# Two more raw weight tiles, a later wait and another order of splits in the first chunk of the last stage

## What is computed

```python
def _merge(x, oa, za, ob, zb, ga, gb, gate, w_br_a, w_br_b, w_out):
    ya = (oa * jax.nn.silu(za)) @ w_br_a
    yb = (ob * jax.nn.silu(zb)) @ w_br_b
    h = jax.nn.sigmoid(ga) * ya + jax.nn.sigmoid(gb) * yb
    return x + gate * (h @ w_out)
...
y_prompt = _rmsnorm(xp) * final_norm_g
y_sample = _rmsnorm(xs) * final_norm_g
```

## Time and profile before

| | |
|---|---|
| median of 3 runs | 1214.68 us (1213.4 to 1214.84) |
| the profiled execution's own time | 1214.08 us |
| its span (first to last instruction) | 1212.3 us |
| PE busy | 1187.5 us, 98% |
| DVE busy | 819.3 us, 68% |
| ACT busy | 601.3 us, 50% |
| POOL busy | 92.4 us, 8% |

### The profile page before, as it was taken

How to read it: one execution, slowest core, us unless ns; L and a number is a source line. 1 busy time by engine, 2 the same in 40 slices (tenths; PEclk the granted TensorE clock), 3 DMA queues, 4 the chain that set the end, 5 groups by cost and what they waited for, 6 DMA issues and landing times.

```text
span 1212.3 us, 19668 instructions
## 1 busy us (share of the span) xinstructions
PE 1187.5 (98%) x7432; PEld 1076.8 (89%) x7432; DVE 819.3 (68%) x1596; ACT 601.3 (50%) x1205; POOL 92.4 (8%) x108
## 2 busy tenths in 40 slices
PE   7999999999999999999999999999999999999998
PEld 1799889989998998899899899989989988998996
DVE  4769458656765776587687597688779966454453
ACT  4632335535552654365465455555547675344342
POOL 0000000000000000000000000000000034533430
PEclk9999999999999999999999999999999999999999
DMA  9547702141123215022511121411113376642540
GB/s 362 178 175 226 231 30 72 45 135 61 40 79 96 64 40 162 22 72 69 139 63 46 49 63 41 134 39 58 38 40 124 113 233 211 204 152 95 201 146 35
DMA packets 71762, 132.81 MB, mean 110 GB/s; under 512 B 6774, under 2 KB 47734, under 8 KB 71676
## 3 DMA queue, kind: packets, MB, share of 16 engines
q1 hardware_dynamic: 57420, 109.70, 28.0%
q10 hardware_dynamic: 14256, 21.96, 5.0%
HBM read 96.24 MB, written 35.40 MB: 109 GB/s over the span
## 4 chain that ended last, share of the span: by engine, by line
PE 84%; DVE 9%; ACT 3%; issue 2%; DMA 1%; POOL 0%; ACTq 0%; SPq 0%; DVEq 0%
PE d_ps_pairs L84 23%; PE s_ps_pairs L84 12%; PE y_ps L1881 9%; PE o_ps_pairs L1070 9%; PE b_ps L84 8%; PE t_ps_pairs L1040 7%; PE v_ps L84 6%; PE s_ps_pairs L1004 4%; PE s_ps_pairs L1003 4%; DMA wada<-in_w_ada 1%; DVE pt L1401 1%; PE k_ps L352 1%; DVE mn L1407 1%; PE t_ps L344 1%; DVE q L1392 1%
## 5 line engine op out<-in xcount | busy, mean ns | idle before, releaser
L84 PE MATMUL d_ps_pairs<-h,wt 128*128 128x384 f32 (+2 forms) x1920 | 352.2, 338 | 0.9 <-ACT craw L1212 0.9
L84 PEld LDWEIGHTS d_ps_pairs<-h,wt 128*128 128x128 f32 x1920 | 316.7, 189 | 16.4 <-ACT craw L1212 1.9
L1401 DVE TENSOR_TENSOR pt<-t_ps_pairs,pt 128x512 fp32r<-128x512 f32 (+2 forms) x264 | 152.9, 619 | 64.7 <-ACT pt L1170 63.5
L84 PE MATMUL s_ps_pairs<-h,wt 128*128 128x512 f32 (+1 forms) x864 | 168.2, 354 | 0.0
L84 PEld LDWEIGHTS s_ps_pairs<-h,wt 128*128 128x128 f32 x864 | 141.6, 189 | 21.7
L1170 ACT ACTIVATE pt<-t_ps_pairs 128x512 fp32r<-128x512 f32 (+2 forms) x264 | 130.2, 544 | 16.8 <-PE t_ps_pairs L1040 11.5
L1194 ACT ACTIVATE pr<-s_ps_pairs,mx 128x896 f32<-128x896 f32 (+1 forms) x128 | 125.0, 982 | 26.9 <-DVE mx L1429 26.5
L1040 PE MATMUL t_ps_pairs<-ident_sb,pr 128*128 128x128 f32 x928 | 125.6, 274 | 1.9 <-DVE pt L1401 1.1
L1881 PE MATMUL y_ps<-wo,mg 128*128 128x512 f32 (+1 forms) x504 | 113.2, 385 | 0.0
L1040 PEld LDWEIGHTS t_ps_pairs<-ident_sb,pr 128*128 128x128 f32 x928 | 105.4, 140 | 8.8 <-DVE pt L1401 5.8
L1881 PEld LDWEIGHTS y_ps<-wo,mg 128*128 128x128 f32 x504 | 91.3, 188 | 20.6
(11 more groups left out here) (204 smaller groups left out, 1588.0 us busy)
## 6 DMA issues: line engine op xcount, KB each, us to landing
wraw<-in_w_gate SPq DMA_DIRECT2D x24, 512.0 KB, 3.8
gt<-gates_d SPq DMA_DIRECT2D x40, 256.0 KB, 4.5
gates_d<-craw ACTq DMA_DIRECT2D x48, 192.0 KB, 1.9
v_d<-vst SPq DMA_DIRECT2D x20, 320.0 KB, 4.6
wada<-in_w_ada SPq DMA_DIRECT2D x12, 512.0 KB, 9.8
oz<-gates_d SPq DMA_DIRECT2D x20, 256.0 KB, 4.6
oz<-o_d SPq DMA_DIRECT2D x20, 256.0 KB, 4.3
x_f<-in_x SPq DMA_DIRECT2D x10, 512.0 KB, 7.0
```

The source lines that it names most:

```text
L84: mm = eng.matmul(out, lhs(a, k), rhs(b, k), start=(k == 0 and i == 0), stop=(k == n_k - 1 and i == 2))
L1401: dve.tensor_tensor(pt[:, 1, c * 512:c * 512 + cols], t_ps[:, n % 2, 0:cols], pt[:, 0, c * 512:c * 512 + cols].bitcast(F32), ALU.subtract) ...
```

## The change

The staging buffers become six: tiles 6 and 7 go into two new ones, `under[:, 1, :]` and `under[:, 3, :]`, which lie over `mg`: the high and the low parts of j = 4 to 7. `stage_of`, `stage_count` and `stage_before` say which buffer a tile has, which load of that buffer it is, and which tile had it before. Tiles 8 to 11 follow tiles 2 to 5, and 12 to 15 follow 8 to 11. SP issues tiles 6, 7 and 8 ahead of the loop, after a new wait for `o_done` (the end of DVE's last work of `pairs`). The wait for the last store moves from before the loop to within j = 4, behind tile 9. In the loop tile 2j + 1 stands ahead of gate tile j and tile 2j + 2 behind it. The lists of splits by turn differ. `gate_in` and `gain_in` share semaphores with the two new buffers, so their counts start one higher.

```diff
+def stage_of(m):
+    return m - 2 if m < 8 else m % 4
+def stage_count(m):
+    return 1 if m < 8 else m // 4
+def stage_before(m):
+    return m - 6 if m < 12 else m - 4
...
 def weight_raw(f, m):
-    return f["stage"][(m - 2) % 4]
+    return f["stage"][stage_of(m)]
...
 def tile_high_f(act, f, m):
-    act.wait_ge(f["w_in"][(m - 2) % 4], ((m - 2) // 4 + 1) * 16)
+    act.wait_ge(f["w_in"][stage_of(m)], stage_count(m) * 16)
...
-    EXTRA = [[4], [5, 6], [7], [8, 9], [10], [11, 12], [13], [14, 15]]
+    EXTRA = [[4], [5], [6], [7, 8], [9, 10], [11, 12], [13, 14], [15]]
...
         def load_w(m):
-            if m >= 6:
-                wait_split(sp, f, m - 4)
+            if m >= 8:
+                wait_split(sp, f, stage_before(m))
...
         load_gt(0, 3)
+        sp.wait_ge(o_done, ALL * STEPS)
         load_w(6)
-        sp.wait_ge(o_out, PAIRS * 32 + 16)
+        load_w(7)
+        load_w(8)
 
         def body(i, first, last):
             for j in range(GSLOTS, KD):
                 if first:
-                    load_w(2 * j - 1)
-                    load_w(2 * j)
+                    load_w(2 * j + 1)
+                    if j == GSLOTS:
+                        sp.wait_ge(o_out, PAIRS * 32 + 16)
                 load_gt(i, j)
+                if first and j < KD - 1:
+                    load_w(2 * j + 2)
             if first:
-                load_w(WT - 1)
...
-                dve.wait_ge(gain_in, 16)
-            dve.wait_ge(gate_in, (i + 1) * 16)
+                dve.wait_ge(gain_in, 32)
+            dve.wait_ge(gate_in, (i + 2) * 16)
...
+        with ExitStack() as early:
+            under = sb(early, "under_mg", [P, 4, D])
         own_f["mg"] = sb(ctx, "mg", [P, 2, KD, CT], F32R)
...
-        own_f.update(wb=wb, wo=wo, stage=[x[:, 0, :], x[:, 1, :], wraw[:, :], craw[:, :]])
+        own_f.update(wb=wb, wo=wo, stage=[x[:, 0, :], x[:, 1, :], wraw[:, :], craw[:, :], under[:, 1, :], under[:, 3, :]])
```

More of the change, by code:

```diff
@@ L1625, in finish_tables @@
     f = dict(own)
-    f["w_in"] = [sem(f"w_in{s}") for s in range(4)]
+    f["w_in"] = [sem(f"w_in{s}") for s in range(6)]
     f["first_in"] = [sem(f"first_in{n}") for n in range(PIECES)]
@@ L1657, in finish @@
     x_in, y_out = [sem("x_in0"), sem("x_in1")], [sem("y_out0"), sem("y_out1")]
-    gate_in, gain_in, eps_set = sem("gate_in"), sem("gain_in"), sem("eps_set")
+    eps_set = sem("eps_set")
+    gate_in, gain_in = w_in[4], w_in[5]
     y_mm, gated, res, sq_done, rms_done, r_done, y_done = (
@@ L1681, in load_w @@
         def load_w(m):
-            if m >= 6:
-                wait_split(sp, f, m - 4)
+            if m >= 8:
+                wait_split(sp, f, stage_before(m))
             src = io["w_br"][m] if m < KD else io["w_out"][:, m - KD, :]
-            sp.dma_start(weight_raw(f, m), src).then_inc(w_in[(m - 2) % 4], 16)
+            sp.dma_start(weight_raw(f, m), src).then_inc(w_in[stage_of(m)], 16)
         def load_oz(i, n):
```

## The result

The changed kernel takes 1220.24 us (median of 6, 1217.58 to 1220.79) against 1214.53 us for the kernel before (6 runs, 1213.24 to 1214.95): +5.7 us, ratio 1.0045 with a 95% interval of 1.0035 to 1.0055. Its profiled execution took 1219.88 us, the span 1218.1.

The account below looks back on a forecast made before the run. TensorE, busy 1187.5 of 1212.3 us, was taken to bound the kernel. The gate-tile loop delays its k=7 by 5.8 us, other parts priced at zero: 1214.68 + 5.8 = 1220.5 us, range 1215.5 to 1224.7.

Parts of the forecast that it names:

- The term that counts: Last stage, chunk 0: gate tiles behind weights that wait for later splits form a serial loop; PE's k=7 +5.8 us.
- Gate 5 lands: Landing of gate tile 5 in chunk 0, taken at 995.0, between 993.5 and 996.5; it was 994.8 before.
- First turn: Gate 5 through sigmoid 5, split 9 and weight 13 to gate 6 landed: 7.2 us, landing at 1002.2.
- Second turn: Gate 6 through sigmoid 6, split 11 and weight 15 to gate 7 landed: 7.2 us, landing at 1009.4.
- Sigmoid 7 to the last low part: Chunk 0, j=7: two splits ahead of product 7 instead of one, so 7.9 us in place of 6.9.
- mg_lo(7) done: Low part of chunk 0's last merged product, done at 1017.4; PE's k=7, which needs it, was at 1011.6.
- signs named for "right": PE waits 1.5 to 2 us before j=6; gates 6, 7 issued near 998, 1005.5; ACT waits over 3; y_ps stops 4 to 6.
- First half of the splits: Chunk 0's branch pass: the 0.88 us wait before j=4 goes and reappears at j=6, gain zero.
- The long sum on GpSimd: GpSimd's sum for j=7 in chunk 0 keeps its long 1.65 us beside a split; short price would give +4.9.
- The moved store wait: SP's `o_out` wait, moved to j=4, costs nothing: it ended by 982.4, when gate tile 4's product ended anyway.
- The early loads: Tiles 6 to 9 issued earlier by SP, but sharing one stream, so landings come earlier only by a little.
- rival "faster": Loads arrive in time, PE loses nothing at k=7: 1212.2 to 1213.8 us, if gate 5 lands by 989.3; chance 0.07.

Follow-up runs that it names:

- e1: Changed kernel with gate tiles 5 to 7 put back ahead of weights 2j+1 and 2j+2 in SyncE's order: 1214.16 us.
- e5: Changed kernel with gate tile 7 alone moved ahead of weight 15 in SyncE's order: 1215.84 us.
- e6: Changed kernel with gate tile 6 alone moved ahead of weight 13 in SyncE's order: 1217.35 us.
- e2: Kernel before with the new order of splits alone, four buffers and SyncE's old order: 1217.05 us.
- x2: Changed kernel with gate tiles first and the old order of splits throughout, keeping six buffers and early loads: 1214.37 us.
- e10: Changed kernel with gate 5 behind weight 10, gates 6 and 7 behind weight 11, ahead of weights 12 to 15, and splits a turn later: 1212.64 us.
- e11: Changed kernel with gate 5 behind weight 10, gates 6 and 7 behind weight 11, ahead of weights 12 to 15, keeping its own splits: 1212.66 us.
- e4: Changed kernel with 16 matmuls added ahead of the wait for k=5 in chunk 0's output pass: 1219.81 us.
- e9: Kernel before with the new order of splits, plus 16 matmuls added ahead of j=7 in chunk 0: 1216.01 us.
- e3: Changed kernel with the old order of splits alone: 1219.42 us.

## Why the prediction was right, point by point

**The term that counts** held in mechanism, and the total was near: 1220.5 forecast, 1220.24 measured. The two turns of the loop are rows of the chain above, and e1, e5 and e6 show that undoing them, both or one, takes back all, most or half. But that the total agrees to 0.3 us is in part luck. The sum came out by errors that cancel, and by the stage the loss was 6.9 us, not 5.8. In us from the stage's start, forecast beside measured:
- Gate 5 lands: 18.7, was 16.5 (991.70 - 975.17). This term was mis-sized by 2.2. I had added one weight's 1.9 us and taken off 1.3 for the earlier start. In fact gate 5 was issued 1.7 us earlier (11.05 in place of 12.72), since weight 11 ahead of it now waits for split 5 only, and it landed after 5.46 us in place of 5.8: the added weight cost nothing visible. The 1.9 us came from a stretch in which the queue was not always full (207 to 352 GB/s in slices of 2 us). In the changed kernel the stream ran at 407 to 417 GB/s from 982 to 986, 1.3 us for 512 KB.
- First turn: 7.2, was 8.9. Split 9's low part took 1.69 us, and gate 6's issue and landing 5.17 in place of 4.0.
- Second turn: 7.2, was 7.6 (1000.59 to 1008.19).
- Sigmoid 7 to the last low part: 7.9, was 7.6 (1008.21 to 1015.83).
- mg_lo(7) done: 41.1, was 40.7.

TensorE's end of chunk 0 then came not 5.8 but 6.3 us late (1029.4 - 975.17 = 54.3 against 1024.26 - 976.27 = 48.0), as TensorE ran at half clock until 1016.9, through k=5 and 6 and past the end of `mg_lo(7)` at 1015.83, which I had not foreseen. Chunk 1's branch pass took 23.6 in place of 23.04, the price put at 0 with 1 as its bound.

Of the signs named for "right", both late issues and both long waits of ScalarE came (gate 6 was issued at 995.40, earlier than the 998 expected), and the stop in `y_ps` was 3.91 us, just short of 4. The wait before j=6 did not come.

**First half of the splits: wrong in place.** I had the wait before j=4 reappear in full before j=6. Sigmoid 4 ran at 988.46, 13.3 us into the stage in place of 15.1, since the early weights and gate 4 did land earlier; product 4 came at 992.35 and j=6 started without a visible wait. The wait reappeared before j=7 instead (1.14 us), for product 5 behind splits 9 and 10, where I had put 0.6. It cost nothing more, since the output pass had to stop later anyway; in e2, without that stop, the wait was 2.15 us and j=7 ran 1.15 us longer at the lower clock.

**The long sum on GpSimd** took its long price again, beside split 15:

```profile
1012.93 1.64 POOL L1854 TENSOR_TENSOR tp<-tp 128x256 f32<-128x256 f32 x1 [0.15 <-DVE tp L1980]
```

The rule of the Trainium skill, "SBUF — State Buffer", section "SBUF: two separate sides", agrees with that row: VectorE's subtraction with two SBUF inputs ran from 1012.76, and GpSimd's sum took 1.64 us in place of 0.73.

**The moved store wait: wrong in its reason.** I had the wait for the last store of `pairs` end by 982.4, no later than product 0, which gate tile 4 needs anyway. With the early loads issued beside it, the store took 5.1 us to land (3.2 before), and SyncE stood for it with gate tile 4 behind it. SyncE's waits in the changed kernel (us in total, times, longest):

```profile
SPq L1717 <- DMA o_d<-ost: 1.9, 1, 1.9
```

It cost no time that the runs can tell: gate tile 4 was still issued 8.1 us into the stage in place of 8.5, and x2, with such a wait of 1.4 us, equals the kernel before. Gate tile 4 ahead of this wait, which the order of e10 does not free either (2.0 us), was not tried.

**The early loads: worth nothing under the old splits.** x2 carries them and equals the kernel before. The rule to issue early and wait late ("DMA: Bandwidth & Descriptors", section "Rules for kernel authors", again of the Trainium skill) held for the weights, but paid only against the price of the new splits (e1 against e2) and nothing beside the kernel before, because the gate tiles were the late ones. Applied to the gate tiles it gave the only gain of the study (e10, e11).

**The rival "faster"** named its own condition, gate 5 landed by 989.3, that is 13.0 us into the stage. Measured 16.5: nearer than I thought, and still out of reach.

## What to carry to other kernels

In a queue that is served in order, ask of every entry what the entries ahead of it wait for, and whether that in turn needs the entry itself; a loop through such a queue takes its whole length at each turn (here 7.6 to 8.9 us), and two more buffers did not shorten it. Put the transfers that many engines wait for ahead of those that have slack, above all ahead of any that must first wait for a buffer that is freed late. And take the price of a transfer from a stretch where the queue was full if the change fills it.

## What the runs showed of the hardware

- TensorE's granted clock fell to 0.50 (1.2 GHz, from 2.4) in the changed kernel during a stop of 3.91 us, and in e2 after a stop of 2.15 us, only 1.5 us after work had resumed; it was low until 5.7 and 4.9 us after work had resumed. In e5, with a wait of 1.38 us, it stayed at 1.00. Sixteen matmuls of no use in the gap kept it at 1.00 in e4 and e9.
- The clock early in the kernel differs between executions of the same work. The stretch from 20 to 40 us before, and then in the changed kernel:

```profile
20.00:40.00 20.00, 16.09 (x63) 5.86 (x64) 16.18 (x27) 14.30 (x18) 0.00 (x0) 0.94 1.04 393
```

```profile
20.00:40.00 20.00, 15.72 (x68) 5.66 (x68) 16.00 (x26) 14.29 (x18) 0.00 (x0) 1.00 1.04 393
```

  0.94 against 1.00. The later stage began 1.1 us earlier in the second. Of all 14 profiles, the five with 1.00 both from 20 to 40 and from 40 to 60 us (changed kernel, e3, e6, e10, e11) began the stage at 974.9 to 975.4, the other nine at 976.3 to 977.1. A change of a few us is therefore better read from the length of its own stage than from times since the span's start.
- The stream from HBM ran at 407 to 417 GB/s with the queue full, against 266 GB/s at 984 to 986 us before, where the queue was partly empty.
- A store landed later when more loads went out beside it: the last store of `pairs` landed after 3.2 to 3.7 us in the four kernels with four buffers, and after 4.6 to 6.2 us in the ten with SyncE's early loads.
- A 256 KB gate tile with one weight issued just ahead of it took 4.0 us to land before, 5.0 in e6 and 5.1 in e1. What makes that 1 us I did not find.
